# Feed-forward's last two output chunks computed by halves of the tokens, with layer 1's first norm split the same way

## The reference, cut to what matters

```python
# layer 0, both streams, each with its own modulation
ctx = ctx + cgt2 * swiglu(modulate(rms_norm(ctx, g_norm2[0]), csh2, csc2), w1, w3, w2)
x   = x   + gt2  * swiglu(modulate(rms_norm(x,   g_norm2[0]), sh2,  sc2),  w1, w3, w2)
# layer 1 (last): the context is needed only for the recurrent part's input columns
hc = modulate(rms_norm(ctx, g_norm1[1]), csh1, csc1)
... hc @ w_in[1][:, C_X_START:C_X_END]        # 512 of the 2304 columns
hx = modulate(rms_norm(x, g_norm1[1]), sh1, sc1)
proj = hx @ w_in[1]                           # all 2304 columns
```

## Time and profile before

| | |
|---|---|
| median of 3 runs | 1561.42 us |
| lowest, highest | 1560.53, 1562.51 us |
| the profiled execution, first to last instruction (its span; no other time of it is given) | 1559.4 us |
| PE busy | 1477.2 us, 95% of the span |
| DVE busy | 838.9 us, 54% |
| ACT busy | 617.5 us, 40% |
| mean granted TensorE clock | 0.977 of full speed |

### The profile page before, as it was taken

One profiled execution on the slowest core, in us unless ns is written; L12 is line 12 of the kernel. 1 busy time (PEld: TensorE's weight loads), 2 busy tenths in 40 slices (PEclk: granted clock), 3 DMA queues, 4 the chain that ended last, 5 costly groups with the idle time before them and its releaser, 6 DMA issues.

```text
span 1559.4 us, 21947 instructions
## 1 busy us (share of the span) xinstructions
PE 1477.2 (95%) x8714; PEld 1041.6 (67%) x8715; DVE 838.9 (54%) x1135; ACT 617.5 (40%) x698; POOL 17.4 (1%) x56
## 2 busy tenths in 40 slices
PE   5999798999999999897879999999999999999997
PEld 3786486788888887783755566565766566565754
DVE  2899945333333333799564554445554555545552
ACT  3425723322122222439344333434443444434442
POOL 2000000000000000100010000000000000000000
PEclk8999899999999999999889999999999999999998
DMA  9633933921542233348159999989999999999992
GB/s 360 199 100 106 363 108 129 236 75 56 146 116 78 69 93 125 102 142 331 49 217 395 340 330 337 343 323 407 381 408 405 403 385 401 408 379 404 383 409 105
DMA packets 208006, 395.44 MB, mean 254 GB/s; under 512 B 12044, under 2 KB 123040, under 8 KB 207904
## 3 DMA queue, kind: packets, MB, share of 16 engines
q1 hardware_dynamic: 207312, 393.80, 70.2%
q10 hardware_dynamic: 592, 0.21, 0.1%
HBM read 392.93 MB, written 1.05 MB: 253 GB/s over the span
## 4 chain that ended last, share of the span: by engine, by line
PE 87%; DVE 4%; ACT 4%; DMA 2%; issue 2%; DVEq 0%; ACTq 0%
PE bank L757 85%; PE bank L1248 1%; DMA raw<-in_w_mod 1%; DMA raw<-in_moe_w 1%; DVE tb L1828 1%; ACT la L1532 1%; DVE y L1957 0%; DVE h_lo L1836 0%; ACT lr L1526 0%; PE bank L1193 0%; DMA rows_sb<-in_b_mod 0%; ACT lm L1574 0%; PE bank L782 0%; ACT li L1528 0%; ACT lm L1539 0%
## 5 line engine op out<-in xcount | busy, mean ns | idle before, releaser
L2265 DVE TENSOR_TENSOR w_lo<-raw,w_hi 128x2048 fp32r<-128x2048 f32 x132 | 302.4, 2292 | 260.5 <-ACT w_hi L1653 260.5
L1653 ACT ACTIVATE w_hi<-raw 128x2048 fp32r<-128x2048 f32 x132 | 252.4, 1912 | 402.1 <-PE bank L757 285.5
L757 PE MATMUL bank<-h_hi,w_hi 128*128 128x512 f32 (+1 forms) x768 | 285.2, 371 | 13.1 <-DVE h_lo L1836 12.0
L757 PE MATMUL bank<-h_lo,w_hi 128*128 128x512 f32 (+1 forms) x768 | 283.0, 368 | 0.0
L757 PE MATMUL bank<-h_hi,w_lo 128*128 128x512 f32 (+1 forms) x768 | 282.9, 368 | 0.0
L1411 ACT ACTIVATE w_hi<-raw 128x2048 fp32r<-128x2048 f32 (+1 forms) x64 | 113.7, 1776 | 209.8 <-PE bank L757 196.0
L757 PEld LDWEIGHTS bank<-h_hi,w_hi 128*128 128x128 f32 x768 | 147.2, 192 | 38.8 <-DVE h_lo L1836 13.4
L757 PEld LDWEIGHTS bank<-h_lo,w_hi 128*128 128x128 f32 x768 | 147.2, 192 | 23.5
L757 PEld LDWEIGHTS bank<-h_hi,w_lo 128*128 128x128 f32 x768 | 146.9, 191 | 23.5
L1811 DVE TENSOR_TENSOR w_lo<-raw,w_hi 128x2048 fp32r<-128x2048 f32 (+1 forms) x64 | 136.0, 2124 | 36.8 <-ACT w_hi L1411 36.6
L757 PE MATMUL bank<-w_hi,hc_hi 128*128 128x512 f32 (+1 forms) x384 | 153.1, 399 | 2.4 <-ACT warm L1708 2.4
(11 more groups left out here) (307 smaller groups left out, 1796.6 us busy)
## 6 DMA issues: line engine op xcount, KB each, us to landing
raw<-in_moe_w SPq DMA_DIRECT2D x220, 1024.0 KB, 9.0
raw<-in_w_mod SPq DMA_DIRECT2D x48, 1024.0 KB, 8.7
raw_x<-in_moe_w SPq DMA_DIRECT2D x44, 1024.0 KB, 8.9
raw<-in_ffn_w SPq DMA_DIRECT2D x44, 512.0 KB, 5.3
raw<-in_w_in SPq DMA_DIRECT2D x18, 1024.0 KB, 5.4
raw<-in_ffn_w SPq DMA_DIRECT2D x16, 704.0 KB, 4.5
raw<-in_w_out SPq DMA_DIRECT2D x8, 1024.0 KB, 5.7
x_in<-in_ctx SPq DMA_DIRECT2D x1, 1024.0 KB, 5.0
```

Source lines behind the costliest of these rows:

```text
L757: return nc.tensor.matmul(dst, lhsT, rhs, start=first, stop=last)
L1653: nc.scalar.activation(w_hi[:, j % SPL, :], raw[:, E_SLOT[j], :], ACT.Copy)\
L2265: V.tensor_tensor(w_lo[:, j % SPL, :], raw[:, E_SLOT[j], :], w_hi[:, j % SPL, :].bitcast(F32), ALU.subtract).then_inc(dve_done, dve_n(name ...
```

## The change

The last two output blocks (d = 6 and 7) are no longer made for all 512 tokens. PE makes them in this order: latent half of block 6, the sums of block 5's squares, latent half of block 7, context half of block 6, the latent sums of blocks 6 and 7, context half of block 7, and then the spreading of the latent inverse root (`last_down`). The context halves go into the second bank of the chunk's pair. ACT, DVE and PE handle layer 1's first norm per stream. The latent stream comes first; the context's blocks 0 to 3 stand behind the splitting of w2, and its blocks 4 to 7 behind the splitting of w3. The new `second_products` takes w0 for the blocks 0 to 3, then w1 for the blocks 0 to 3, then both for the blocks 4 to 7, and has the context's sums and its spreading in between. The `hi` and `low` of w1 and w2 move from behind the `down` blocks into the norm; layer 1's shifts and amplitudes (`modulated`, `amplitude`) move in front of the two blocks.

```diff
-NORM_SPLIT = {(0, 2): ORD[("w_out", 0, NWOUT - 1)], (1, 1): ORD[("down", 1, KD - 1)]}
+NORM_SPLIT = {(0, 2): ORD[("w_out", 0, NWOUT - 1)]}
...
+            def last_down():
+                two = [("down", 1, d) for d in (KD - 2, KD - 1)]
+                taken = [take(c) for c in two]
+                for s in (1, 0):
+                    for c, (w, banks) in zip(two, taken):
+                        for k in range(KG):
+                            i = split_mm(banks[1 - s][:, tok(s)], (w[0][:, P * k:P * k + P], w[1][:, P * k:P * k + P]),
+                                         (f_hi[:, k, tok(s)], f_lo[:, k, tok(s)]), k == 0, k == KG - 1)
+                        i.then_inc(pe_done, pe_n("mm_x" if s else "mm", ORD[c]))
+                        if (s, c[2]) == (1, KD - 2):
+                            mean_square(1, 1, slice(0, T), [KD - 3])
+                        elif (s, c[2]) == (0, KD - 2):
+                            half_square(1, KD - 2)
+                            half_square(1, KD - 1)
+                half_root(1)
...
+            def second_products():
+                for n in range(2):
+                    for k in range(4):
+                        pe.wait_ge(dve_done, at("h_lo", 1, 1, k, 1))
+                        if k == 0:
+                            take(("w_in", 1, WIN_ORDER[n]))
+                        for t in range(2):
+                            product(1, n, t, k)
+                for k in range(4, KD):
+                    pe.wait_ge(dve_done, at("h_lo", 1, 1, k, 1))
+                    for t in range(2):
+                        for n in range(2):
+                            product(1, n, t, k)
+                    if k == 4:
+                        for d in (KD - 2, KD - 1):
+                            half_square(0, d)
+                    if k == 6:
+                        half_root(0)
...
# ACT, layer 1
+                    for d in (KD - 2, KD - 1):
+                        half_square(1, d)
+                    half_root(1)
+                    for d in range(3):
+                        half_high(1, d)
+                    hi(ORD[("down", 1, KD - 2)] + SPL)
+                    half_square(0, KD - 2)
+                    for d in range(3, 5):
+                        half_high(1, d)
+                    half_square(0, KD - 1)
+                    for d in range(5, KD):
+                        half_high(1, d)
+                    act.wait_ge(pe_done, at("mm", ORD[("down", 1, KD - 1)]))
+                    hi(ORD[("down", 1, KD - 1)] + SPL)
+                    half_root(0)
+                    for d in range(4):
+                        half_high(0, d)
                 s0, s1 = ORD[("w_in", l, 0)], ORD[("w_in", l, 1)]
                 for t in range(2):
                     act.wait_ge(pe_done, at("mm" if t else "half", s0))
                     if t:
                         hi(s0 + SPL)
+                        if l == 1:
+                            for d in range(4, KD):
+                                half_high(0, d)
                     nc.scalar.activation(tb[:, t, ts], bank[2 * (s0 % 3) + t][:, ts], ACT.Copy)\
                         .then_inc(act_done, act_n(*(("evac", s0) if t else ())))
...
# DVE, layer 1
+                    for d in (KD - 2, KD - 1):
+                        down_add(1, d, 1)
+                    half_inverse(1)
+                    dve.wait_ge(pe_done, at("rs", 1, 1, 1))
+                    half_normed(1, range(2))
+                    down_add(1, KD - 2, 0)
+                    half_normed(1, range(2, 4))
+                    low(ORD[("down", 1, KD - 2)] + SPL)
+                    down_add(1, KD - 1, 0)
+                    half_normed(1, range(4, KD))
+                    half_inverse(0)
+                    low(ORD[("down", 1, KD - 1)] + SPL)
+                    dve.wait_ge(pe_done, at("rs", 1, 1, 0))
+                    half_normed(0, range(4), 3)
...
                 low(s0 + SPL)
+                if l == 1:
+                    half_t(0, 4)
+                    half_normed(0, range(4, KD))
```

More of the change, by code:

```diff
@@ L1044, in _ @@
                                 columns(*m)
-                    for d in range(KD):
+                    for d in range(KD if g == 0 else KD - 2):
                         c = ("down", g, d)
@@ L1631, in _ @@
                         act.wait_ge(pe_done, at("mm", s))
-                        if s not in LATE_SPLIT:
-                            hi(s + SPL)
+                        hi(s + SPL)
+                squares(1, 1, slice(0, T), ("down", 1), [KD - 3])
             h_high(1, 2, (1,), hT, "h")
@@ L1932, in _, with down_add @@
             amplitude(0, 1)
+            def down_add(g, d, s):
+                s0 = ORD[("down", g, d)]
+                name = ("xT", "down", g, d) if s == 1 else ()
+                if g == 1 and d >= KD - 2:
+                    dve.wait_ge(pe_done, at("mm_x" if s else "mm", s0))
+                    name = ("xT", "down", g, d, s)
+                b = bank[2 * (s0 % 3) + (g == 1 and d >= KD - 2 and s == 0)]
+                V.scalar_tensor_tensor(xT[:, d, tok(s)], b[:, tok(s)], modT[:, 0, 40 + d, s:s + 1],
+                                       xT[:, d, tok(s)], ALU.mult, ALU.add).then_inc(dve_done, dve_n(*name))
             for l in range(2):
@@ new lines, in half_t, with half_low @@
+                def half_t(s, d):
+                    if d >= 2:
+                        dve.wait_ge(act_done, at("h_hi", 1, 1, d - 2, s))
+                        dve.wait_ge(dve_done, at("h_lo", 1, 1, d - 2, s))
+                    V.scalar_tensor_tensor(tb[:, d % 2, tok(s)], xT[:, d, tok(s)], amp[:, 1, 0, d, s:s + 1],
+                                           rs_of(s), ALU.mult, ALU.mult).then_inc(dve_done, dve_n("t", 1, 1, d, s))
+                def half_low(s, d):
+                    dve.wait_ge(act_done, at("h_hi", 1, 1, d, s))
+                    V.scalar_tensor_tensor(h_lo[:, d, tok(s)], tb[:, d % 2, tok(s)], modT[:, 1, d, s:s + 1],
+                                           h_hi[:, d, tok(s)].bitcast(F32), ALU.add, ALU.subtract)\
+                        .then_inc(dve_done, dve_n("h_lo", 1, 1, d, s))
@@ new lines, in half_normed @@
+                def half_normed(s, blocks, last=KD - 1):
+                    for d in blocks:
+                        if d == 0:
+                            half_t(s, 0)
+                        if d < last:
+                            half_t(s, d + 1)
+                        half_low(s, d)
+                if l == 1:
+                    for d in (KD - 2, KD - 1):
[12 more added lines that the diff above has]
+                    half_normed(0, range(4), 3)
@@ L2186, in _ @@
                         for s in range(2):
[L2187 to L2193, removed]
+                            down_add(g, d, s)
+                        low(s0 + SPL)
+                modulated(1, 0, 2)
+                amplitude(1, 1)
             inverse_rms(1, 2)
```

58 lines of the change are left out of this document (48 added, 10 removed).

## The result

The changed kernel takes 1569.45 us (median of 4 runs, 1568.01 to 1569.80) against 1561.80 us (1560.53 to 1562.51, 4 runs) before: a ratio of 1.0049, 95% interval 1.0036 to 1.0062. It is slower by 7.65 us, and the forecast of 1565.7 us, with a range to 1568.5, was too low. The direction and the wait that takes the gain back were as forecast; the price was not.

A forecast was written before the change was run, and what follows sets the result against it. PE, busy for 95% of the span, was taken as the bound. A later start of w3 (+2.3 us) and the slow clock (+2.0 us) summed to +4.3 us, 1565.7 us, range 1561.5 to 1568.5.

The forecast's parts named there:

- Smaller products, +1.4 us: Last feed-forward blocks: 66 matmuls become 132 of 256 tokens, +0.9 us, and a second group of sums adds +0.56.
- First product at 630.5: Layer 1's first product starts at 630.5 in place of 635.0, -4.5 us.
- w1's splitting ends at 636.8: In the latent norm, w1's `w_lo` of 2.29 us follows `h_lo` of block 3 and ends at 636.8.
- w2 at 646.7: In layer 1's projection, w2 starts at 646.7 in place of 650.5, -3.8 us.
- w3 at 658.6, behind ACT's copy: After PE idles 6.1 us for ACT's copy of w0's second half, w3 starts at 658.6, +2.3 us.
- The clock, 0.5 + 1.5 us: Slow clock costs 0.5 us behind the shorter waits (636.8 on) and 1.5 behind the 6.1 us wait before w3.
- Nothing caught up: From w3 to w8 neither PE nor DVE can catch up; at least 2.4 us would arrive behind w8.
- the one with the slow clock in both stretches: Slow clock costs 2.0 us behind each stretch of waits, and a late rise once more: 1568 us, chance 0.14.
- The two rivals at or below the time of before: At w3: no wait, 1557.7 us, chance 0.07; or only the copy early, -1.4 us, 1560.0 us, chance 0.06.

The follow-up runs named there:

- both kernels with these waits filled: Changed kernel plus 32 idle matmuls in the latent norm's waits, without or with 50 more ahead of w3: 1570.65 us and 1564.30 us.
- both waits filled: Changed kernel plus 32 idle matmuls in the latent norm's waits and 50 in the wait ahead of w3: 1564.30 us, ratio 1.0015.
- first waits filled: Changed kernel plus 32 idle matmuls of 256 columns in PE's waits of the latent norm: 1570.65 us, ratio 1.0056.
- sums early: Changed kernel with the context's sums of blocks 6 and 7 behind w1's block 1 and its spreading behind block 5 on PE: 1568.95 us, ratio 1.0048.
- the copies-first run: Changed kernel with ACT's copies of w0 and w1 and w4's `w_hi` ahead of the context's blocks 4 to 7: 1562.81 us, ratio 1.0008.
- v1: Changed kernel's seam reordered on PE, ACT and DVE, with fewer convolution taps ahead of w4's splitting: 1562.53 us, ratio 1.0005 to the kernel before.
- w3's wait filled: Changed kernel plus 50 idle matmuls of 256 columns in PE's wait ahead of w3: 1566.25 us, ratio 1.0031.
- the two with early sums: Changed kernel with the context's sums earlier on PE, alone or with ACT's copies of w0 and w1 also moved ahead: 1568.95 us and 1562.25 us.
- the changed kernel's second profile: The changed kernel measured once more, nothing edited: 1569.63 us, ratio 1.0046.

## Why the prediction fell short

By its own steps, in its clock (a time of after plus 1.47 us):

- **Smaller products, +1.4 us.** From the sums in front of block 6 to the end of the feed-forward's last slot it measured 17.58 us against 16.03, +1.55. Right. The row also decides between the trace's 13 ns above the columns' time and the 2.5 ns of the Trainium skill, "TensorE: Matmul & The Clock Gate", section "Wait — 56ns, not 53.3ns?": with the latter it would have been, by estimate, some 0.8.
- **First product at 630.5.** 629.35 + 1.47 = 630.8. Right, with a wait of 1.63 us. **w1's splitting ends at 636.8:** 637.1. Right.
- **w2 at 646.7.** 649.5. Here it went wrong. At full clock it is right: both kernels with these waits filled have w2 at 36.0 behind block 5, which is 647.1.
- **w3 at 658.6, behind ACT's copy.** The mechanism is as told, a wait of 6.67 us (forecast 6.1) ended by the row named. The time is 662.1. At full clock it would be 48.6 + 611.1 = 659.7, so 1.1 us of the miss are a chain of ACT and DVE that I took too short, 0.4 of it in the end of w2's `w_hi` (642.2 for 641.8), and 2.4 us are the clock.
- **The clock, 0.5 + 1.5 us.** This is the step that failed. The second number is nearly right (7.77 - 5.76 = 2.0 us on w3). The first was 0.5 and is 2.4 us in the trace. I took the low stretch for short, since products break the waits up; it lasted 10.2 us, against 6.8 us at the seam before. And I charged it to PE's products alone, with the context's sums as part of PE's sum for w2, though ACT's root, the head of the chain that sets w3, waits for them: 2.55 us in place of none. Clock and wait were treated as two terms, where one drives the other. Together the clock cost 5.2 us in time (both waits filled; 4.3 of them show at w5) where 2.0 stood in the sum: 3.2 of the 3.75 us that are missing from 1565.7, or 2.3 of them by the trace.
- **Nothing caught up.** Right: w4's splitting starts at 664.1 in place of 656.3 and the one behind w8 at 100.1 in place of 92.3, 7.8 us at both, and 7.65 us arrive in the median.

The nearest rival was the one with the slow clock in both stretches, 1568 us, which I gave 0.14. It had the sizes of the low stretches as +2.0 each, and that is close to what they were. The Trainium skill, "TensorE: Matmul & The Clock Gate", section "HAM oscillation — how this bites in real kernels", says that bursts with long waits between them start cold each time. The wait ahead of w3 agrees: wherever PE had no work in it for over 6 us, the clock fell (both profiles of the changed kernel, first waits filled, sums early). The stretch with the short waits agrees in both profiles of the changed kernel, but not in every kernel, as the last section shows. The rival should still have had the larger chance. The two rivals at or below the time of before needed the copy and the splitting early; the copies-first run, with only the copy early and the first half clock still in it, shows what that gives: 1.0008, +1.0 us against the kernel measured beside it, where the rival had -1.4.

## What to carry to other kernels

- When work is moved ahead of an engine's copy out of PSUM, find who waits for that copy: here the context's blocks of the norm, ahead of the copy, made PE wait 6.7 us, and a change of ACT's order alone took 6.6 us of time back.
- A wait of PE has a second price in the clock behind it, and it must be run through every chain that starts from a product made there, not added at the end. Idle matmuls in the waits test this: here they took 5 us off, though one of the two sets alone took nothing off. Better still is an order without the waits.
- Gains at a seam are given back by whatever was deferred to make them. v1 won 5.4 us and paid them with 14 taps behind w8; the same order with the taps in their place kept 3.9 us (1561.53 - 1557.68).

## What the hardware showed that I had not expected

The first half clock of the seam doesn't come in every execution of the same instructions. Up to the products of w1, PE's stream is the same in the changed kernel, in the one with w3's wait filled, in the copies-first one and in the two with early sums. The clock fell 21.3 to 21.5 us behind block 5 in the first three (and in the changed kernel's second profile), and it stayed up in the last two. PE had done the same until then in all six profiles: a wait of 1.63 or 1.64 us in front of layer 1's first product, which starts 19.7 us behind block 5. The waits behind that point are longer where the clock stayed up (1.02 and 1.27 us in the sums-early run against 0.34 and 0.60 in the changed kernel), since PE is through with each block sooner. Same stretch, sums early, then the changed kernel again:

```profile
631.50:640.50 9.00, 6.51 (x50) 5.49 (x50) 7.58 (x15) 5.30 (x10) 1.59 (x1) 1.00 0.26 73
```

```profile
631.50:640.50 9.00, 7.88 (x34) 7.12 (x33) 6.91 (x12) 5.31 (x9) 0.68 (x1) 0.50 0.38 111
```

The fall comes before the first instruction that differs, so it isn't the edit's doing. The Trainium skill, "TensorE: Matmul & The Clock Gate", section "What's actually happening", calls the count of slow matmuls at a kernel's start run-variable; these profiles show the like in the middle of one.

The mean granted clock of each whole execution tells more than the single profiles, though it doesn't say where the clock was low. By estimate, 10.2 us at half clock lower it by 5.1 / 1568 = 0.003. With only w3's wait filled, ten executions of the same code fall apart in two: six have 0.977 to 0.980 and spans of 1562.7 to 1564.7 us, the other four 0.973 to 0.976 and 1565.4 to 1568.5. The profiled one, with the fall, is among the four. That fits a fall that comes in some executions and costs about 3 us where it does. The sums-early kernel has 0.975 in the profiled execution and 0.972 or 0.973 in the other six, so its profile, the one without the fall, is likely the exception, and its median is not the time of what the trace shows.

It stays open why the run with only the first waits filled did not get faster: its four executions have 0.974 to 0.976, above the changed kernel's usual 0.972, and the pause at 1375.59 explains only the profiled one. The run with both sets filled, which contains it, has no such loss (1561.9 - 705.87 = 856.0 us from the splitting behind w8 on).
